# Scatter of the experts' results: gates moved from the selection matrix into split results

## What is computed

```python
gate = jax.nn.softmax(top_logit, axis=-1) * g_w[:, None]      # [256 tokens, 2]
...
def run_block(args):
    xblk, e = args
    hid = jax.nn.silu(xblk @ w1[e]) * (xblk @ w3[e])          # 1024 -> 512
    return hid @ w2[e]                                        # 512 -> 1024
...
y = jnp.zeros((T + 1, D)).at[slot_tok].add(yb * slot_w[:, None])[:T]
```

## Time and profile before

| | us |
|---|---|
| median of 3 executions | 1603.47 (1602.63 to 1615.23) |
| the profiled execution, its own time | 1611.56 |
| its span, first to last instruction | 1609.6 |
| busy PE / DVE / ACT | 1525.9 / 712.9 / 566.0 |
| mean granted clock of PE, share of full | 0.959 |

### The profile page before, as it was taken

One profiled execution on the slowest core, in us unless ns is written; L12 is line 12 of the kernel. 1 busy time (PEld: TensorE's weight loads), 2 busy tenths in 40 slices (PEclk: granted clock), 3 DMA queues, 4 the chain that ended last, 5 costly groups with the idle time before them and its releaser, 6 DMA issues.

```text
span 1609.6 us, 26565 instructions
## 1 busy us (share of the span) xinstructions
PE 1525.9 (95%) x11398; PEld 1250.1 (78%) x11398; DVE 712.9 (44%) x1137; ACT 566.0 (35%) x883; POOL 28.0 (2%) x47
## 2 busy tenths in 40 slices
PE   5899999899998989999999899989899999999997
PEld 3898899899998658999999778979656556556563
DVE  3657757766777425554446535644211111111110
ACT  1531244344444434544445735543111111212111
POOL 1000000000001001000000000001000000000000
PEclk8899999999989889999999879999999999999999
DMA  9668635989769403455554223716699999999992
GB/s 330 196 214 288 232 132 186 327 285 321 269 213 336 157 0 125 162 187 183 178 155 132 84 76 103 288 53 252 271 416 419 423 422 421 422 424 421 420 424 96
DMA packets 175635, 404.15 MB, mean 251 GB/s; under 512 B 5013, under 2 KB 139442, under 8 KB 163250
## 3 DMA queue, kind: packets, MB, share of 16 engines
q1 hardware_dynamic: 173504, 397.43, 66.6%
q0 software_dynamic: 1648, 5.18, 1.1%
q10 hardware_dynamic: 386, 0.11, 0.0%
HBM read 401.63 MB, written 1.07 MB: 250 GB/s over the span
## 4 chain that ended last, share of the span: by engine, by line
PE 87%; DVE 6%; DMA 3%; ACT 3%; issue 1%; SPq 0%; ACTq 0%; DVEq 0%
PE ps L1750 28%; PE ps L2268 14%; PE ps L2290 7%; PE ps L1981 7%; PE ps L1763 4%; PE ps L1785 4%; PE ps L2255 4%; PE ps L2300 4%; PE ps L2013 2%; PE ps L1914 2%; PE ps L1838 2%; DMA arena<-in_mod_w 2%; PE ps L1848 1%; DVE wsplit L1119 1%; PE ps L1805 1%; DMA arena<-in_b_w_q 1%
## 5 line engine op out<-in xcount | busy, mean ns | idle before, releaser
L1750 PE MATMUL ps<-u,wsplit 128*128 128x256 f32 x3912 | 485.3, 285 | 8.6 <-DVE wsplit L1119 7.1
L1750 PEld LDWEIGHTS ps<-u,wsplit 128*128 128x128 f32 x3912 | 477.0, 193 | 15.9 <-DVE wsplit L1119 8.1
L1119 DVE TENSOR_TENSOR wsplit<-arena,wsplit 128x1024 fp32r<-128x1024 f32 x258 | 312.6, 1224 | 250.4 <-ACT wsplit L739 247.4
L739 ACT ACTIVATE wsplit<-arena 128x1024 fp32r<-128x1024 f32 x258 | 270.6, 1056 | 332.2 <-PE ps L1750 161.4
L1676 DVE TENSOR_TENSOR arena<-arena,ps 128x256 f32<-128x256 f32 x32 | 13.5, 421 | 358.6 <-ACT arena L1085 358.6
L2268 PE MATMUL ps<-arena 128*64 128x256 f32 x1408 | 155.7, 379 | 0.8 <-DVE arena L1671 0.8
L2268 PEld LDWEIGHTS ps<-arena 128*64 128x64 f32 x1408 | 101.0, 137 | 60.6 <-issue 12.0
L1981 PE MATMUL ps<-hid,wsplit 128*128 128x256 f32 x1056 | 130.2, 283 | 0.3 <-DVE hid L1360 0.3
L1981 PEld LDWEIGHTS ps<-hid,wsplit 128*128 128x128 f32 x1056 | 128.2, 192 | 0.5 <-DVE hid L1360 0.5
L1091 ACT ACTIVATE arena<-ps 64x512 f32<-64x512 f32 x64 | 37.8, 591 | 154.0 <-PE ps L2290 153.2
L1763 PE MATMUL ps<-u,wsplit 128*128 128x256 f32 x528 | 73.6, 304 | 14.6 <-DVE u L1168 12.8
(11 more groups left out here) (345 smaller groups left out, 1375.8 us busy)
## 6 DMA issues: line engine op xcount, KB each, us to landing
arena<-in_w SPq DMA_DIRECT2D x66, 2048.0 KB, 17.0
late<-in_w SPq DMA_DIRECT2D x30, 2048.0 KB, 17.2
arena<-in_mod_w SPq DMA_DIRECT2D x48, 1024.0 KB, 6.9
arena<-in_ffn_w_in SPq DMA_DIRECT2D x44, 1024.0 KB, 5.5
arena<-in_ffn_w_out SPq DMA_DIRECT2D x22, 1024.0 KB, 4.9
arena<-in_a_w_in SPq DMA_DIRECT2D x16, 1024.0 KB, 7.9
arena<-in_kv_mod_w SPq DMA_DIRECT2D x8, 1024.0 KB, 5.3
arena<-in_kv_w SPq DMA_DIRECT2D x8, 1024.0 KB, 7.2
```

The source lines that it names most:

```text
L739: act.activation(piece_buf(p, 0), piece_src(p), ACT.Copy).then_inc(hi_done, 1)
L1119: dve.tensor_tensor(piece_buf(p, 1), piece_src(p), piece_buf(p, 0).bitcast(F32), ALU.subtract).then_inc(lo_done, 1)
L1750: mm = pe.matmul(o, w_[:, k, :], u[:, x_, k, :], start=first, stop=last)
```

## The change

The gates leave the matrix. The transposed gate matrix stays in PSUM, and DVE makes two things of it (`slot_gates`): `slot_gate`, one number a slot (the row's maximum), and `slot_token`, the same matrix with 1 where the gate was, in float32r. The results are multiplied by the slot's gate and split: ACT writes the high part (`results_hi`), DVE the low part (`results_lo`), both into `y_split`, in float32r. The scatter is then `slot_token` by the high and by the low part: two float32r matmuls where one float32 matmul stood. PE now waits for `results_lo` (`m_yl`) in place of `m_yc`. ACT's copy of the transposes is 256 columns wide for every expert. `y_split` and `slot_token` lie where `h` and `sq` end their life; `masks`, `h` and `sq` have other places in SBUF.

The diff, cut (the branch for more than 64 tokens at an expert has the same edits, and is not entered with these inputs):

```diff
-            def expert_act(n, k, with_gates):
+            def expert_act(n, k):
...
-                w = 512 if with_gates else 256
-                act.activation(tt[:, 0:w], ps[:, 1, 0:w], ACT.Copy).then_inc(m_tc, 1)
+                act.activation(tt, ps[:, 1, 0:256], ACT.Copy).then_inc(m_tc, 1)
...
+            def results_hi(n, pair):
+                act.wait_ge(m_gr, pair + 1)
+                act.wait_ge(m_yc, 2 * n + 2)
+                act.activation(y_split[:, 0, :], y_sb, ACT.Copy, scale=slot_gate).then_inc(m_yh, 1)
...
+            def slot_gates(n):
+                dve.wait_ge(m_tc, n + 1)
+                dve.tensor_reduce(out=slot_gate, in_=ps[:, 1, 256:512], axis=AX, op=ALU.max).then_inc(m_gr, 1)
+                dve.tensor_scalar(slot_token[:], ps[:, 1, 256:512], 0.0, None, ALU.is_gt)
+
+            def results_lo(pair):
+                dve.wait_ge(m_yh, pair + 1)
+                dve.scalar_tensor_tensor(out=y_split[:, 1, :], in0=y_sb, scalar=slot_gate,
+                                         in1=y_split[:, 0, :].bitcast(F32), op0=ALU.mult, op1=ALU.subtract)\
+                    .then_inc(m_yl, 1)
...
-            def scatter(copied, rows=2 * CAP, blocks=range(TB)):
-                pe.wait_ge(m_yc, copied)
+            def scatter(pairs_done, rows=2 * CAP, blocks=range(TB)):
+                pe.wait_ge(m_yl, pairs_done)
                 for b in blocks:
                     for j in range(2):
-                        mm = pe.matmul(ps[:, 2 + 2 * b + j, :], tt[0:rows, 256 + P * b:256 + P * (b + 1)],
-                                       y_sb[0:rows, 512 * j:512 * (j + 1)], start=False, stop=False,
-                                       skip_group_check=True)
+                        for x_ in range(2):
+                            mm = pe.matmul(ps[:, 2 + 2 * b + j, :], slot_token[0:rows, P * b:P * (b + 1)],
+                                           y_split[0:rows, x_, 512 * j:512 * (j + 1)], start=False, stop=False,
+                                           skip_group_check=True)
```

More of the change, by code:

```diff
@@ L229, in two_blocks @@
         late = sb("late", [P, RING * SLOT + DC * T])
-        h = sb("h", [P, DC, T])
-        sq = sb("sq", [P, DC, T])
         vec1 = sb("vec1", [P, 112])
@@ L244, in two_blocks @@
         small = sb("small", [P, 3, 64])
+        masks = sb("masks", [P, 8, P], U8)
+        with ExitStack() as until_experts:
+            h = until_experts.enter_context(nc.sbuf_tensor("h", [P, DC, T], F32))
+            sq = until_experts.enter_context(nc.sbuf_tensor("sq", [P, DC, T], F32))
+        y_split = sb("y_split", [P, 2, D], F32R)
+        slot_token = sb("slot_token", [P, T], F32R)
         def vec(name, i=0):
@@ L408, in two_blocks @@
         GATE, (HALF1,), (HALF0,) = jobs["w_gate"], jobs["w_half1"], jobs["w_half0"]
-        masks = sb("masks", [P, 8, P], U8)
         xor_i = part(12288, 3, P)
@@ L545, in two_blocks @@
         m_yc = sem("m_yc")
+        m_gr = sem("m_gr")
+        m_yh = sem("m_yh")
+        m_yl = sem("m_yl")
         m_all = sem("m_all")
@@ L552, in two_blocks @@
         xe = part(14336, DC, 2 * CAP)
-        tt = part(15360, 512)
+        tt = part(15360, 256)
+        slot_gate = part(15616, 1)
         y_sb = part(15872, D)
@@ L1092, in expert_act @@
                                    ACT.Copy).then_inc(m_yc, 1)
+            def results_hi(n, pair):
+                act.wait_ge(m_gr, pair + 1)
+                act.wait_ge(m_yc, 2 * n + 2)
+                act.activation(y_split[:, 0, :], y_sb, ACT.Copy, scale=slot_gate).then_inc(m_yh, 1)
             with act.Fori(0, NE // 2) as i:
                 for k in range(2):
-                    expert_act(2 * i + k, k, k == 1)
+                    expert_act(2 * i + k, k)
+                results_hi(2 * i + 1, i)
             act.wait_ge(m_flag, 1)
@@ L1101, in _ @@
                     for p_ in range(3):
-                        expert_act(3 * e + NE + p_, 0, True)
+                        expert_act(3 * e + NE + p_, 0)
+                        results_hi(3 * e + NE + p_, 3 * e + NE // 2 + p_)
                 act.wait_ge(m_all, 1 + 3 * NE)
@@ L1698, in _ @@
                 tokens(i + 1, 0)
+                slot_gates(2 * i + 1)
                 tokens(i + 1, 1)
+                results_lo(i)
                 hidden_e(2 * i + 2)
@@ L1704, in _ @@
             tokens(NE // 2 - 1, 0)
+            slot_gates(NE - 3)
             tokens(NE // 2 - 1, 1)
+            results_lo(NE // 2 - 2)
             hidden_e(NE - 2)
@@ L1708, in _ @@
             hidden_e(NE - 1)
+            slot_gates(NE - 1)
+            results_lo(NE // 2 - 1)
             dve.wait_ge(m_flag, 1)
@@ L1719, in _ @@
                         hidden_e(3 * e + NE + p_)
+                        slot_gates(3 * e + NE + p_)
+                        results_lo(3 * e + NE // 2 + p_)
                 dve.wait_ge(m_all, 1 + 3 * NE)
@@ L2312, in middle @@
                 elif k == 0:
-                    scatter(2 * n, blocks=(0,))
+                    scatter(3 * i + at // 2, blocks=(0,))
                 turn_e(n, k == 1)
@@ L2318, in middle @@
                 elif k == 0:
-                    scatter(2 * n, blocks=(1,))
+                    scatter(3 * i + at // 2, blocks=(1,))
                 down(n, w_, loaded)
@@ L2335, in _ @@
                 middle(4, n - 24, follows=n < NE - 1)
-            scatter(2 * NE).then_inc(m_all, 1)
+            scatter(NE // 2).then_inc(m_all, 1)
             pe.wait_ge(m_flag, 1)
@@ L2347, in _ @@
                         down(n, 0, 16 * e + 16 * (NE // 3 + 2))
-                        scatter(2 * n + 2, CAP).then_inc(m_all, 1)
+                        scatter(3 * e + NE // 2 + p_ + 1, CAP).then_inc(m_all, 1)
 _INPUTS = ["x", "c", "mod_w", "mod_b", "norm_mix", "norm_ffn", "ffn_w_in", "ffn_w_out", "a_w_in", "a_w_out",
```

## The result

Over 20 executions of each, the changed kernel takes a median of 1599.62 us (1588.44 to 1608.61) and the kernel before 1609.51 us (1601.48 to 1619.02). The ratio is 0.9939, with a 95% interval of 0.9922 to 0.9957: 9.8 us less (7.0 to 12.6). A second comparison, with fewer executions, gives 0.9940 (0.9914 to 0.9967). The change makes the kernel faster by 0.6%, which is within 1%.

A forecast was written before the change was run, and what follows sets the result against it. PE was taken to set the experts' pace, with the weight stream binding after the change. 15.2 us gained less 0.8 lost at the end made 14.4 off 1603.47: 1589.1 us, range 1580.5 to 1597.

The forecast's parts named there:

- What bounded the kernel before: Experts' stage: PE sets the pace at 14.52 us an expert; the full DMA stream is hidden by a 15.1 us lead.
- What the change takes from PE: Scatter in the experts: 1.5 us a pair saved, over fifteen pairs 22.5 us that PE alone would gain.
- What is late next: Experts' weight loads: PE catches up some six experts before the end; the last half `up` begins 15.0 us earlier.
- Rival (b): Experts' stage: the clock falls once PE waits for loads; two falls near the end give 1592.6 us; chance 0.09.
- The end of the program: Behind the last `down`: 2.46 us more chain, 1.70 less scatter, together a loss of 0.8 us (0.5 to 1.0).
- The absolute time: Whole kernel: 14.4 us off the median of 1603.47, giving 1589.1 us.
- (a): Experts' loads: the stream runs faster than in the trace, PE stays the bound; 21.9 us gain, 1581.6 us; chance 0.20.
- (c): Scatter matmuls: not done in one pass; at four passes 16 pairs add 55 us, 1658 us; chance 0.02.
- (d): DMA stream: suffers from added traffic or deeper queue; at 5% slower, near 1611 us; chance 0.05.
- (e): High and low part take twice as long: hidden in the stage, 2.4 us more lost at the end, 1591.5 us.

The follow-up runs named there:

- e2: Kernel before with a quarter of each scatter left out (last 512 columns of tokens 128 to 255): stage 452.4 us, ratio 0.9903 to the kernel before.
- e3: Kernel before with the loads of w2 for experts 3 to 31 halved: stage 466.1 us, ratio 0.9994 to the kernel before.
- e4: Changed kernel with the loads of w2 for experts 3 to 31 halved: stage 445.5 us, ratio 0.9863 to the kernel before.
- e6: Changed kernel with four unread float32 matmuls in PE's wait ahead of the last scatter: stage 452.2 us, one execution.
- e9: The changed kernel once more, unaltered: stage 453.0 us, ratio 0.9940 to the kernel before.
- e7: Changed kernel with the last pair scattered as before the change (plain float32, no split): stage 451.3 us, ratio 0.9899 to the kernel before.
- e1: Kernel before with only masks, h and sq moved to the change's places in SBUF: stage 466.1 us, ratio 1.0008 to the kernel before.
- e5: Changed kernel with two more ACT passes of 128x1024 ahead of each high part: stage 456.2 us, one execution.

## Why the prediction was right or wrong

**What bounded the kernel before: right.** PE set the pace with full DMA engines behind it, and the stream would bind once PE lost more than its lead. e2 (a relief under the lead, 13.7 us for 13.8 expected), e3 (the stream relieved, nothing) and e4 (the stream relieved under the change, 7.9 us) show it.

**What the change takes from PE: right.** 1.5 us a pair was taken, 1.53 measured; the pairs run at 27.50 us as announced. (The prediction's lower bound of 1.46 for the scatter should read 1.49: eight records of 0.243 and 0.2 for the starts make 2.14.)

**What is late next: right in kind, 0.5 us too high.** The last w3 was to land 432.6 us after the first load, it landed after 433.1. The second half of the last `up` starts 451.5 us after the first `up` before, and 437.1 after: 14.5 us for 15.0. PE had caught up six experts before the end, the pairs went to 29.8 us, and the clock did not fall in those waits. The waits for `down` that the prediction also named did not come. Rival (b) drew on the clock gate's rule in the Trainium skill ("TensorE: Matmul & The Clock Gate", "HAM oscillation — how this bites in real kernels"). The loop that this section describes waits longer for its DMA than it computes. Here the waits are 0.5 to 1.2 us in 14.9, and the trace shows 1.00 throughout the loop; so the prediction's "most of the gain would go" asked more of the rule than its case bears. Behind the wait of 3.9 us at the end the clock did fall.

**The end of the program: the term that was mis-sized.** This is the step that failed in the sum. It had a loss of 0.8 us there, split as 2.46 more chain and 1.70 less scatter; measured it is a loss of 1.9. The chain cost 2.56. The scatter gave 0.70, not 1.70, since the clock fell behind the wait that the chain opens. With work in that wait (e6) it would have given 1.58; the other 0.12 are records of 0.247 us where 0.23 was taken. The prediction named the low clock and left it out of the sum. So the stage is shorter by 14.5 + 0.1 - 2.6 + 0.7 = 12.7 us. After the first output copy another 8.2 us pass (7.6 in e9) where it was 6.3 before, with the output's transfers landing 4.4 us after issue (4.1) in place of 3.2. That leaves 10.8 us, 11.8 in e9, from the first `up` to the last instruction. The prediction had no term for this part, and set it at nothing without a reason. Whether it is the change's doing is open: e7 has 6.3 us there, and e2, a kernel of the old kind, 7.8.

**From 11 to 9.8 us.** The timed 9.8 (7.0 to 12.6) holds the 11.3 that the two profiles give on average. The rest would fit the slightly lower mean clock (0.956 in both timings of the change, 0.959 to 0.961 in those of the kernel before). Whether that is chance or something that the change brings about ahead of the experts stays open. The twelve profiles show no such cost: the first `up` starts at 1135 to 1142 us in the four of the old kind (mean 1137.7) and at 1125 to 1145 in the eight of the new (mean 1134.9). e1 shows no price of the places in SBUF, but its interval is wider than the gap of 1.5 us.

**The absolute time: wrong by its base, the second step that failed.** 14.4 us were taken from 1603.47, the median of three. The median over twenty is 1609.5, and in the three later comparisons it is 1610.0, 1610.3 and 1611.8. Taken from 1609.5, the forecast would have been 1595.1, with the measured 1599.6 4.5 us above. The profile had hinted at it: the profiled execution took 1611.56, and the prediction set its 8.1 us aside. Executions of the kernel before spread from 1601.5 to 1619.0 us; the median of three of them was 6 us off, and the range had no room for that.

**The rivals.** (a) a faster stream: no, the last landing did not move, and no slice reached 435 GB/s, the ceiling by the Trainium skill ("DMA: Bandwidth & Descriptors", "Where 436 GB/s comes from"); the fullest slice of either profile has 425. The same section of the Trainium skill gives about 358 GB/s as what binds transfers between HBM and SBUF, which these loads are; the traces are well above it, at 416 to 425. (The range's lower end, 1580.5, was called (a)'s, but (a)'s own sum is 1581.6.) (c) more passes a matmul: no, eight records took 2.12 us in e6 at full clock; less 0.39 for the last one (the shortest of these records in e5's profile is 387 ns long), the other seven take 0.247 each, just over the upper bound (0.243). (d) a stream slowed by the change: no, by 0.1%. (e) a chain exposed in the loop: no, by e5.

## What to carry to other kernels

When an engine and the DMA queues are both full, measure the lead of the loads: the time between a load's landing and its use at the end of the stage is the most that a relief of the engine can bring there as long as the stream itself stays as it is (14.5 us here, for a lead of 15.1). Steps that are free inside a loop since the next item covers them are paid in full behind the last item, so the last item may deserve the old form. And take a forecast's base from as many executions as there are; where the clock falls in some executions and not in others, compare stages of profiles, not spans.

## What the runs showed of the hardware that was not expected

- With many loads outstanding, issuing one is no longer short. In the changed kernel a DMA instruction of SyncE takes 0.33 us at 1293.48, 9.53 at 1416.28 and 13.66 at 1486.87, while some seven loads of 2 MB wait (the last w2 lands 37.1 us after its issue, at 5 us a load). In the kernel before, no such instruction takes over 0.5 us between 1380 and 1560. It should cost nothing here, since the stream is full and SyncE has nothing else to do, but another DMA that SyncE had to issue there would have come later; no run tests this.
- A wait of 3.9 us of PE ahead of the last scatter was followed by matmuls at the low clock, part of them in the change and e9 (3.00 and 2.97 us for eight) and all of them in e4 (3.78 us after 3.87) and in e5 (3.78 us after 5.94), while waits of 0.5 to 1.2 us in four of the last five experts left it at 1.00. In the change the clock read 1.00 through the whole wait and fell only once the matmuls ran again.
- A part of the stages before the experts runs at 1.2 GHz in some executions and at 2.4 GHz in others of the same kernel, for up to 31 us between 545 and 579. In seven of the twelve profiles the low clock holds there for 27 to 31 us, in four for less, and in that of the change not at all. This alone makes 10.5 us of the difference between the profiles before and after.
